# Order of the products inside a pair of experts in the first layer's MoE block

## The chip, the cores and the metric

The kernel runs on one core of a Trainium2 chip. The metric is the device time of one execution in microseconds (us), lower is better. The engines named below are TensorE (PE, matrix products and transposes), VectorE (DVE), ScalarE (ACT), GpSimd (POOL) and SyncE (SP, which here only issues loads of weights). Each engine works through its own program in the order in which it is written and meets the others at semaphores.

## The reference

A trunk of two layers over 256 latent tokens and 256 context tokens of 1024 channels. Each layer has four token mixers and then a mixture of experts (16 experts, each token goes to two of them). The context tokens go through the experts in the first layer only. What the change touches is the block of one expert:

```python
def expert_block(args):
    xblk, e = args
    u = jax.nn.silu(xblk @ w1[e]) * (xblk @ w3[e])
    return u @ w2[e]
```

with `w1` and `w3` of 1024 x 512 and `w2` of 512 x 1024, all in float32 (2048 KB each).

## The kernel before

**The experts of the first layer.** The 16 experts are taken two at a time, in 8 pairs `e`. A pair works on a main block of 64 rows (tokens) per expert and on a side block of 32 further rows per expert. The main block is multiplied by `both_halves`: the even expert's 64 rows stand in one half of the array's columns and the odd expert's in the other (L1515 and L1517, so those two lines alternate in the trace). The side block is multiplied by `four_quarters` (L1525), four products of 32 columns at a time. The first layer has the side block (`side` is true), the second has none, and takes other branches everywhere.

**A pair on PE, before:** gate product of the main block (PSUM bank 2), gate product of the side block (bank 7), up product of the main block (bank 3), up product of the side block (bank 6), then `turn_u` (four transposes of the main inner rows `u`, L1585), the low half of the down product (needs `uT`, the turned rows copied to SBUF), `turn_side_u` (L1591), the high half, and the side block's down product. PE's loop over pairs is unrolled.

**A pair on the other engines.** These programs are not in the diff. DVE: `activated` (L2718), `side_activated` (L2723 and L2725), `hidden` (L2731, writes the main inner rows and signals `u_ready`), `side_hidden` (L2735, L2738), the turning of the next pair's tokens (L2145, L2151), the results. ACT: `tanh` (L1944), `side_parts` (L1950 copies one half of the side gate product and waits for `side_gate_done`; L1952 is its tanh and waits for DVE's sum; L1954 copies one half of the side up product and waits for `side_up_done`), `turned_u` (L1958 copies the turned rows and signals `uT_ready`), the results and their stores.

**The weights.** Each of the six matrices of a pair has one place in SBUF: a place in the ring and one beside it (`n_` for `w1`, `hT` for `w3`, `wide` for `w2`). SP's loop waits for the last reader of a matrix kind, then issues the two loads of the next pair:

```python
def last_reader(w, l):
    if with_side(l):
        return {"w1": side_gate_done, "w3": side_up_done, "w2": side_down_done}[w]

for w in ("w1", "w3", "w2"):
    sp.wait_ge(last_reader(w, l), base + e)
    sp.dma_start(at[w][0], pairs_of[w][l, e, 0]).then_inc(at[w][1], 16)
    sp.dma_start(odd_at[w], pairs_of[w][l, e, 1]).then_inc(odd_landed[w], 16)
```

**The token rows** of pair `e + 1` are gathered by POOL while pair `e` is worked on.

Of the kernel before, what the change touches and what calls it, by code (L numbers as in the profile page):

```python
# [149 lines left out]
def with_side(l):  # L150

    return live(l) == TILES
# [477 lines left out]
def build_trunk(nc, xin, ccol, crows, const, cols, rows, hfw, wr, wmod, win, wbr, wout, w1, w3, w2, out):  # L630
    with ExitStack() as ctx:
# [3 lines left out]
        def sem(name):  # L635
            return ctx.enter_context(nc.semaphore(name))
# [19 lines left out]
        side_xT = yT[:, 1, 0, :].rearrange("p (k n) -> p k n", n=HALF)  # L656
# [196 lines left out]
        side_xT_ready = sem("side_xT_ready")  # L853
        side_gate_done = sem("side_gate_done")
# [11 lines left out]
        side_y_ready = sem("side_y_ready")  # L866
# [31 lines left out]
        def chunk3(name, n=KD):  # L898
            return chunk(name).rearrange("p (k n) -> p k n", k=n)
# [42 lines left out]
        def odd3(w, n=KD):  # L942

            return odd_at[w].rearrange("p (k n) -> p k n", k=n)
# [14 lines left out]
        def behind_first(l, e):  # L959

            return l or not isinstance(e, int) or e
# [168 lines left out]
        def _(pe):  # L1130
# [10 lines left out]
            for n, name in enumerate(STEPS["T"]):  # L1141
                kind, l, rest = name[0], name[1], name[2:]
# [107 lines left out]
                elif kind == "fdft":  # L1250
                    (j,) = rest
                    pe.wait_ge(vector_done, vector("fnorms", l))
                    side = 256 * (j // 2)
# [199 lines left out]
                elif kind == "experts":  # L1453
# [5 lines left out]
                    side = with_side(l)  # L1459
                    inner = u if side else eth  # L1460
                    wg, wu, wd = chunk3(("w1", l)), chunk3(("w3", l)), chunk3(("w2", l), 4)
                    wg2, wu2, wd2 = odd3("w1"), odd3("w3"), odd3("w2", 4)
# [4 lines left out]
                    def weights_landed(w, e):  # L1467
                        for two in range(2):
                            if l and ("w2", e, two) in LAST_W2 and w == "w2":
                                continue  # L1470
                            if l:
                                pe.wait_ge(*home_landed((w, e, two)))
                            elif two:
                                pe.wait_ge(odd_landed[w], e * 16 + 16)
                            else:
                                pe.wait_ge(place[w], first[w] + e * 16)
# [5 lines left out]
                    def of_pair(w, e):  # L1482
                        if l:
                            return [home_slices((w, e, two)) for two in range(2)]
                        return slices(fourths(chunk((w, l))), KD), slices(fourths(odd_at[w]), KD)
# [26 lines left out]
                    def both_halves(bnk, left, even, odd):  # L1512
                        n_k = len(even)
                        for k in range(n_k):
                            pe.matmul(ps[0:HALF, bnk, :], left[:, k, 0:HALF], even[k],  # L1515
                                      start=(k == 0), stop=(k == n_k - 1), skip_group_check=True)
                            last = pe.matmul(ps[HALF:P, bnk, :], left[:, k, HALF:P], odd[k],  # L1517
                                             start=(k == 0), stop=(k == n_k - 1), skip_group_check=True)
                        return last

                    def four_quarters(bnk, left, quarters):

                        for k in range(4):
                            for g, (weights, k0, rows_, cols_) in enumerate(quarters):
                                last = pe.matmul(ps[SIDE * g:SIDE * (g + 1), bnk, :], left[:, k0 + k, rows_:rows_ + SIDE],  # L1525
                                                 weights[:, k0 + k, cols_], start=(k == 0), stop=(k == 3),
                                                 skip_group_check=True)
                        return last

                    def split_k(even, odd):  # L1530
                        whole = slice(0, FE)
                        return [(even, 0, 0, whole), (odd, 0, SIDE, whole), (even, 4, 0, whole), (odd, 4, SIDE, whole)]
# [11 lines left out]
                    def mix(e):  # L1544

                        if not e:
                            pe.wait_ge(pieces_ready, l + 1)
                        pe.wait_ge(mixing_ready, e + 1)
                        pe.wait_ge(y_low, base + e + 1)
                        pe.wait_ge(y_high, base + e + 1)  # L1550
                        mix_block(e == 0, e == PAIRS - 1).then_inc(y_mixed, 1)

                    def gate_and_up(e):

                        pe.wait_ge(turned_low, base + e + 1)
                        if not e:
                            pe.wait_ge(turned_high, l + 1)
                        if behind_first(l, e):
                            pe.wait_ge(u_ready, base + e)
                            if side:  # L1560
                                pe.wait_ge(side_uT_ready, e)
                            if not side:
                                pe.wait_ge(y_low, base + e)
                        weights_landed("w1", e)
                        both_halves(2, xgT, *of_pair("w1", e)).then_inc(gate_done, 1)
                        if side:
                            pe.wait_ge(side_xT_ready, e + 1)
                            if behind_first(l, e):
                                pe.wait_ge(side_y_ready, e)
                            four_quarters(7, side_xT, split_k(wg, wg2)).then_inc(side_gate_done, 1)  # L1570
                        if not side and e:
                            mix(e - 1)
                        weights_landed("w3", e)
                        if not side:
                            pe.wait_ge(y_high, base + e)
                        both_halves(3, xgT, *of_pair("w3", e)).then_inc(up_done, 1)
                        if side:
                            if behind_first(l, e):
                                pe.wait_ge(y_high, base + e)
                            four_quarters(6, side_xT, split_k(wu, wu2)).then_inc(side_up_done, 1)  # L1580

                    def turn_u(e):
                        pe.wait_ge(u_ready, base + e + 1)
                        for f in range(4):
                            last = pe.transpose(ps[:, u_bank, f * P:(f + 1) * P], inner[:, f * P:(f + 1) * P], ident)  # L1585
                        last.then_inc(u_turned, 1)
# [8 lines left out]
                    def down(e):  # L1595
                        pe.wait_ge(uT_ready, base + e + 1)
                        weights_landed("w2", e)
                        if behind_first(l, e):
                            pe.wait_ge(y_low, base + e)
                        last_columns_landed(e, last_low)  # L1600
                        even, odd = of_pair("w2", e)
                        both_halves(low_bank, uT, even[0::2], odd[0::2]).then_inc(down_low, 1)
                        if side:
                            turn_side_u(e)
                        if behind_first(l, e):
                            pe.wait_ge(y_high, base + e)
                        last_columns_landed(e, last_high)
                        both_halves(high_bank, uT, even[1::2], odd[1::2]).then_inc(down_high, 1)
                        if side:
                            pe.wait_ge(side_uT_ready, e + 1)  # L1610
                            low, high = slice(0, FE), slice(FE, D)
                            four_quarters(7, side_uT, [(wd, 0, 0, low), (wd2, 0, SIDE, low), (wd, 0, 0, high),
                                                       (wd2, 0, SIDE, high)]).then_inc(side_down_done, 1)

                    def pair(e):
                        gate_and_up(e)
                        turn_u(e)
                        if side and not e:
                            pe.wait_ge(pieces_ready, l + 1)
                        down(e)  # L1620
# [25 lines left out]
                    for e in range(PAIRS):  # L1646
                        pair(e)
# [1330 lines left out]
```

## Time and profile before

| | |
|---|---|
| time, median of 3 runs (lowest to highest) | 1540.88 us (1540.47 to 1541.53) |
| time of the profiled execution | 1544.08 us |
| its span, first to last instruction | 1542.1 us |
| mean granted clock of TensorE in it | 0.989 |
| first layer's pairs of experts, from the first gate product to the end of the last side product | 663.3 to 933.1 us |
| PE busy over the span | 1445.8 us (94%) |
| DVE, ACT, POOL busy over the span | 757.9, 277.6, 165.9 us |

The profiled execution is 3.2 us above the median of the runs. The span leaves out what lies before the first and behind the last instruction. PE's busy time counts a pipelined product until its modelled end, so consecutive products overlap in the rows; the distance from one start to the next is what a product takes. Two products whose rows start together run side by side in different columns of the array.

### The profile page before, as it was taken

The numbers are of one execution on the slowest core, as the hardware profiler recorded it, in microseconds if no ns is written. First come the engines' busy times: TensorE is split into PE (matmuls) and PEld (weight loads), VectorE is DVE, ScalarE is ACT, GpSimd is POOL, SyncE is SP. The second block draws the span as 40 slices with busy tenths as digits, with TensorE's granted clock in tenths as the row PEclk, the third lists the DMA queues.
The fourth block names the chain that finished last, engine by engine and source line by source line (L and its number), as shares of the span: only waits on it lengthen the run. The fifth ranks groups of instructions, "written<-read, shape, count | busy, mean of one in ns | idle before, by whom it ended". The sixth has DMA issues, their size and how long they took to land. (4 is left out here: it accounts for less than half of the span.)

```text
span 1542.1 us, 17006 instructions
## 1 busy us (share of the span) xinstructions
PE 1445.8 (94%) x6200; PEld 718.8 (47%) x6200; DVE 757.9 (49%) x1689; ACT 277.6 (18%) x570; POOL 165.9 (11%) x156
## 2 busy tenths in 40 slices
PE   6999999789999999999999999899989999999987
PEld 2544644344444444632323233765777875433332
DVE  4297866646555879532122223686676635211112
ACT  3201101422232210411011011110242203000000
POOL 0000011001011210021111101001001210111000
PEclk9999999989999999999999999999999999999999
DMA  9420234101223453689999986425333695999996
GB/s 380 186 98 27 74 145 164 55 28 55 82 82 141 164 191 109 275 322 420 423 425 422 418 360 237 162 85 225 127 110 137 220 374 211 379 418 412 422 420 238
DMA packets 49536, 355.55 MB, mean 231 GB/s; under 512 B 6288, under 2 KB 6672, under 8 KB 22704
## 3 DMA queue, kind: packets, MB, share of 16 engines
q1 hardware_dynamic: 41360, 330.79, 54.3%
q0 software_dynamic: 4800, 14.24, 2.5%
q10 hardware_dynamic: 3296, 9.44, 1.6%
q8 instruction: 52, 0.85, 0.2%
q14 instruction: 28, 0.23, 0.0%
HBM read 343.88 MB, written 10.56 MB: 230 GB/s over the span
## 5 line engine op out<-in xcount | busy, mean ns | idle before, releaser
L1209 PE MATMUL ps<-hT,ring 128*128 128x512 f32 (+1 forms) x1344 | 452.6, 492 | 1.9 <-DVE hT L2334 1.3
L1209 PEld LDWEIGHTS ps<-hT,ring 128*128 128x128 f32 x1344 | 253.8, 192 | 177.0 <-issue 157.9
L1515 PE MATMUL ps<-ring,m 128*64 128x512 f32 x624 | 277.1, 595 | 12.7 <-ACT m L1958 8.0
L1515 PEld LDWEIGHTS ps<-ring,m 128*64 128x64 f32 x624 | 81.9, 137 | 185.4 <-issue 172.7
L2296 DVE SCALAR_TENSOR_TENSOR spare<-ring,crow 128x1024 bf16<-128x1024 f32 x120 | 155.8, 1298 | 4.1
L1222 PE MATMUL ps<-ring,hT 128*128 128x512 f32 (+1 forms) x352 | 125.1, 515 | 0.0
L2021 POOL TENSOR_TENSOR wide<-wide,gates 128x512 f32<-128x512 f32 (+1 forms) x48 | 69.6, 1450 | 395.9 <-DVE gates L2473 395.9
L1517 PE MATMUL ps<-n_,m 128*64 128x512 f32 x224 | 100.0, 595 | 0.0
L1310 PE MATMUL ps<-yT,ring 128*128 128x512 f32 (+1 forms) x256 | 94.5, 492 | 2.3 <-ACT n_ L1857 2.3
L1517 PE MATMUL ps<-wide,m 128*64 128x512 f32 x208 | 93.7, 597 | 0.0
L1222 PEld LDWEIGHTS ps<-ring,hT 128*128 128x128 f32 x352 | 66.7, 190 | 55.1 <-issue 51.4
L1517 PE MATMUL ps<-hT,m 128*64 128x512 f32 x208 | 91.9, 595 | 0.0
L2059 POOL DMA_INDIRECT m<-h_scratch,m x56 | 53.1, 949 | 348.2 <-DVE m L2145 266.5
L1393 PE MATMUL ps<-ring,wide 128*128 128x512 f32 x192 | 83.1, 593 | 1.4 <-issue 1.1
L1816 ACT ACTIVATE gates<-ps,hbg 128x512 f32<-128x512 f32 (+1 forms) x64 | 37.2, 581 | 235.3 <-PE ps L1209 149.8
L2718 DVE SCALAR_TENSOR_TENSOR m<-m,ps 128x512 f32<-128x512 f32 x16 | 11.0, 688 | 134.7 <-ACT m L1944 134.7
L2383 DVE SCALAR_TENSOR_TENSOR n_<-n_,col 128x512 f32<-128x512 f32 (+1 forms) x120 | 74.2, 619 | 4.3
L2473 DVE SCALAR_TENSOR_TENSOR gates<-gates,ps 128x512 f32<-128x512 f32 (+1 forms) x48 | 26.6, 554 | 75.1 <-PE ps L1310 67.8
L2731 DVE TENSOR_TENSOR m<-m,ps 128x512 f32<-128x512 f32 x16 | 11.0, 688 | 104.0 <-PE ps L1517 104.0
L1310 PEld LDWEIGHTS ps<-yT,ring 128*128 128x128 f32 x256 | 45.8, 190 | 32.1 <-issue 24.2
L1525 PE MATMUL ps<-ring,yT 128*32 128x512 f32 x256 | 58.1, 595 | 0.0
L1393 PEld LDWEIGHTS ps<-ring,wide 128*128 128x128 f32 x192 | 36.2, 190 | 46.3 <-issue 46.1
(389 smaller groups left out, 1699.3 us busy)
## 6 DMA issues: line engine op xcount, KB each, us to landing
ring<-w SPq DMA_DIRECT2D x39, 2048.0 KB, 11.1
ring<-win SPq DMA_DIRECT2D x52, 1024.0 KB, 4.9
ring<-wmod SPq DMA_DIRECT2D x48, 1024.0 KB, 5.0
n_<-w SPq DMA_DIRECT2D x13, 2048.0 KB
hT<-w SPq DMA_DIRECT2D x13, 2048.0 KB, 16.6
wide<-w SPq DMA_DIRECT2D x13, 2048.0 KB
ring<-wbr SPq DMA_DIRECT2D x8, 1024.0 KB, 4.8
ring<-wout SPq DMA_DIRECT2D x4, 2048.0 KB, 11.9
```

The costliest lines, as they stand in the source:

```text
L1209: last = pe.matmul(b[:, 0:W], w[:, k, jj * P:(jj + 1) * P], hT[:, k, 0:W], start=(k == 0), stop=(k == KD - 1))
L1222: last = pe.matmul(b[:, 0:wid], hT[:, k, t * P:(t + 1) * P], chunk3(parts[k // ks], ks)[:, k % ks, 0:wid], start=(k == 0), stop=(k == KD - 1))
L1310: last = pe.matmul(b[:, 0:W], w[:, k, j * P:(j + 1) * P], yT[:, bi in (1, 2), k, 0:W], start=(k == 0), stop=(k == 1))
L1393: last = pe.matmul(b, acc[:, k, t * P:(t + 1) * P], w[:, k, :], start=(k == 0), stop=(k == KD - 1))
L1515: pe.matmul(ps[0:HALF, bnk, :], left[:, k, 0:HALF], even[k], start=(k == 0), stop=(k == n_k - 1), skip_group_check=True)
L1517: last = pe.matmul(ps[HALF:P, bnk, :], left[:, k, HALF:P], odd[k], start=(k == 0), stop=(k == n_k - 1), skip_group_check=True)
L1525: last = pe.matmul(ps[SIDE * g:SIDE * (g + 1), bnk, :], left[:, k0 + k, rows_:rows_ + SIDE], weights[:, k0 + k, cols_], start=(k == 0), st ...
L1816: last = act.activation(gth[:, g % 2, 0:W], bank(("gate", l, bi, j))[:, 0:W], ACT.Tanh, bias=hbg[:, bi * 8 + j:bi * 8 + j + 1], scale=0.5)
L2021: last = nc.gpsimd.tensor_tensor(acc[:, j, 0:W], acc[:, j, 0:W], gtmp[:, g % 2, 0:W], ALU.add)
L2059: gp.indirect_dma_start(out=xg[:, 256 * g:256 * (g + 1)], out_offset=None, in_=h2_pieces, in_offset=bass.IndirectOffsetOnAxis(ap=pieces[:, ...
L2296: last = v.scalar_tensor_tensor(out=spare[:, 0, :].bitcast(BF16), in0=chunk3(cn, 2)[:, block_ % 2, :], scalar=0.5, in1=crow[:, s, :], op0= ...
L2383: last = v.scalar_tensor_tensor(out=o, in0=ud[:, j, 0:ns, k:k + 256], scalar=w(k), in1=o, op0=ALU.mult, op1=ALU.add)
```

## The change

Only PE's program changes, and only where `side` is true. Inside a pair the main block's gate and up products now come one after the other, ahead of the side block's gate product, and `turn_u` moves from behind the side block's up product to a place between the side gate product and the side up product. The waits go with their steps.

```diff
@@ gate_and_up(e)
                         weights_landed("w1", e)
                         both_halves(2, xgT, *of_pair("w1", e)).then_inc(gate_done, 1)
-                        if side:
-                            pe.wait_ge(side_xT_ready, e + 1)
-                            if behind_first(l, e):
-                                pe.wait_ge(side_y_ready, e)
-                            four_quarters(7, side_xT, split_k(wg, wg2)).then_inc(side_gate_done, 1)
                         if not side and e:
                             mix(e - 1)
                         weights_landed("w3", e)
@@
                         both_halves(3, xgT, *of_pair("w3", e)).then_inc(up_done, 1)
                         if side:
+                            pe.wait_ge(side_xT_ready, e + 1)
+                            if behind_first(l, e):
+                                pe.wait_ge(side_y_ready, e)
+                            four_quarters(7, side_xT, split_k(wg, wg2)).then_inc(side_gate_done, 1)
+                        if side:
+                            turn_u(e)
                             if behind_first(l, e):
                                 pe.wait_ge(y_high, base + e)
                             four_quarters(6, side_xT, split_k(wu, wu2)).then_inc(side_up_done, 1)
@@ pair(e)
                         gate_and_up(e)
-                        turn_u(e)
+                        if not side:
+                            turn_u(e)
                         if side and not e:
                             pe.wait_ge(pieces_ready, l + 1)
                         down(e)
```

PE's program in the second pair of the first layer, before: the first row of each product with what it waits for, in the order gate, side gate, up, side up, turn, down.

```order
L1515 MATMUL ps<-ring,m 64x512 [waits chunk_landed4,side_uT_ready,odd_w1_landed,u_ready,turned_low]
...
L1525 MATMUL ps<-ring,yT 32x512 [waits side_y_ready,side_xT_ready]
...
L1515 MATMUL ps<-ring,m 64x512 [waits odd_w3_landed,chunk_landed0]
...
L1525 MATMUL ps<-ring,yT 32x512 [waits y_high]
...
L1585 MATMUL ps<-con,m 128x128 [waits u_ready]
L1585 MATMUL ps<-con,m 128x128 x3
L1515 MATMUL ps<-ring,m 64x512 [waits odd_w2_landed,y_low,chunk_landed2,uT_ready]
```

The same place in the changed kernel, where `turn_u` is line 1586.

```order
L1515 MATMUL ps<-ring,m 64x512 [waits chunk_landed4,side_uT_ready,odd_w1_landed,u_ready,turned_low]
...
L1515 MATMUL ps<-ring,m 64x512 [waits odd_w3_landed,chunk_landed0]
...
L1525 MATMUL ps<-ring,yT 32x512 [waits side_y_ready,side_xT_ready]
...
L1586 MATMUL ps<-con,m 128x128 [waits u_ready]
L1586 MATMUL ps<-con,m 128x128 x3
L1525 MATMUL ps<-ring,yT 32x512 [waits y_high]
...
L1515 MATMUL ps<-ring,m 64x512 [waits odd_w2_landed,y_low,chunk_landed2,uT_ready]
```

The side gate product moved behind the up product, and the transposes with their wait for `u_ready` now stand directly behind the side gate product and ahead of the side up product.

DVE's program in a pair, in the changed kernel. Its rows are those of before (744 to 748 there too, with line numbers lower by two).

```order
L2720 SCALAR_TENSOR_TENSOR m<-m,ps 128x512 [waits tanh_ready]
L2725 TENSOR_TENSOR gates<-ps,gates 64x512 [waits side_gate_part]
L2727 SCALAR_TENSOR_TENSOR mr<-mr,gates 64x512 [waits side_tanh]
L2733 TENSOR_TENSOR m<-m,ps 128x512 [waits up_done,gate_ready]
L2737 TENSOR_TENSOR gates<-ps,mr 64x512 [waits side_up_copied]
```

The fourth row signals `u_ready`. Nothing moved here: it still stands behind the two rows that need the side gate product.

ACT's program in a pair, in the changed kernel, again as before but for the line numbers.

```order
L1946 ACTIVATE m<-ps 128x512 [waits gate_done]
L1952 ACTIVATE gates<-ps 64x512 [waits side_gate_done]
L1954 ACTIVATE mr<-gates 64x512 [waits side_gate_sum]
L1956 ACTIVATE mr<-ps 64x512 [waits side_up_done]
L1960 ACTIVATE m<-ps 128x512 [waits u_turned]
```

The last row signals `uT_ready`, on which the down product waits. It still stands behind the copy that needs the side up product.

## Rows read from the trace of the kernel before

**Rows 1.** Busy time by stretch, two of the pairs: PE, PEld, DVE, ACT, POOL, clock, DMA

```profile
core 0: us, PE busy (x) PEld busy (x) DVE busy (x) ACT busy (x) POOL busy (x), PEclk, DMA share, GB/s
697.30:731.10 33.80, 33.05 (x202) 10.09 (x200) 7.58 (x12) 3.61 (x6) 5.68 (x6) 1.00 1.01 423
866.10:899.80 33.70, 32.95 (x202) 10.09 (x200) 7.56 (x12) 3.61 (x6) 0.00 (x0) 1.00 1.00 422
```

**Rows 2.** Waits of PE in pairs 2 to 8 (697 to 934 us)

```profile
engine line waited for: us in total, times, longest us
PE ps L1515 <- ACT m L1958: 5.2, 7, 0.7
```

**Rows 3.** Timeline of PE, seventh pair: first product of each step

```profile
start us, us, engine line op out<-in xcount [idle before <-releaser]
865.64 0.64 PE L1515 MATMUL ps<-ring,m 128*64 128x512 f32 x1
...
872.66 0.62 PE L1525 MATMUL ps<-ring,yT 128*32 128x512 f32 x1
...
876.23 0.64 PE L1515 MATMUL ps<-ring,m 128*64 128x512 f32 x1
...
883.25 0.62 PE L1525 MATMUL ps<-ring,yT 128*32 128x512 f32 x1
...
886.82 0.66 PE L1585 MATMUL ps<-con,m 128*128 128x128 f32 x4
888.22 0.64 PE L1515 MATMUL ps<-ring,m 128*64 128x512 f32 x1 [0.75 <-ACT m L1958]
...
899.35 0.64 PE L1515 MATMUL ps<-ring,m 128*64 128x512 f32 x1
```

**Rows 4.** Timeline of ACT, seventh pair

```profile
876.37 0.59 ACT L1950 ACTIVATE gates<-ps 64x512 f32<-64x512 f32 x1 [2.99 <-PE ps L1525]
877.71 0.63 ACT L1952 ACTIVATE mr<-gates 64x512 f32<-64x512 f32 x1 [0.75 <-DVE gates L2723]
886.95 0.59 ACT L1954 ACTIVATE mr<-ps 64x512 f32<-64x512 f32 x1 [8.62 <-PE ps L1525]
887.57 0.60 ACT L1958 ACTIVATE m<-ps 128x512 f32<-128x512 f32 x1
```

**Rows 5.** Timeline of DVE, seventh pair

```profile
876.99 0.68 DVE L2723 TENSOR_TENSOR gates<-ps,gates 64x512 f32<-64x512 f32 x1 [2.90 <-ACT gates L1950]
878.37 0.68 DVE L2725 SCALAR_TENSOR_TENSOR mr<-mr,gates 64x512 f32<-64x512 f32 x1 [0.69 <-ACT mr L1952]
883.43 0.69 DVE L2731 TENSOR_TENSOR m<-m,ps 128x512 f32<-128x512 f32 x1 [4.38 <-PE ps L1517]
```

**Rows 6.** Loads of weights by SP: issues in the seventh pair, then landing times, all pairs

```profile
876.50 0.33 SPq L1074 DMA_DIRECT2D ring<-w  x1
...
886.95 0.33 SPq L1074 DMA_DIRECT2D ring<-w  x1
...
899.48 0.33 SPq L1074 DMA_DIRECT2D ring<-w  x1
...
DMA to landing us min/median/max: 7.9/10.8/11.6
...
DMA to landing us min/median/max: 15.6/16.4/17.3
```

**Rows 7.** Timeline of PE: a transpose behind a wait for DVE's inner rows, second layer

```profile
1357.43 0.66 PE L1585 MATMUL ps<-con,m 128*128 128x128 f32 x4 [1.23 <-DVE m L2731]
```

**Rows 8.** Timeline of PE: the first product behind some of its longest waits

```profile
10.10 1.94 PE L1157 MATMUL ps<-ring,cc 128*32 128x512 f32 x8 [4.02 <-DMA ring<-wmod]
...
307.82 1.29 PE L1331 MATMUL ps<-m 32*128 32x256 f32 x4 [4.71 <-ACT n_ L1857]
...
935.41 2.46 PE L1168 MATMUL ps<-con 128*128 128x512 f32 x4 [2.27 <-issue]
...
1504.86 0.61 PE L1515 MATMUL ps<-ring,m 128*64 128x512 f32 x1 [2.56 <-DMA hT<-w]
```

**Rows 9.** Busy time by stretch, behind these waits (columns as in Rows 1)

```profile
10.10:13.50 3.40, 2.95 (x16) 0.40 (x16) 1.13 (x4) 1.70 (x2) 0.00 (x0) 1.00 1.05 432
307.82:312.00 4.18, 4.18 (x8) 1.98 (x9) 2.70 (x8) 1.59 (x5) 0.00 (x0) 0.50 0.00 0
...
936.63:940.04 3.41, 3.41 (x14) 0.60 (x16) 0.50 (x3) 0.00 (x0) 0.94 (x1) 0.51 0.00 0
...
1504.86:1508.30 3.44, 3.44 (x16) 1.40 (x18) 0.00 (x0) 0.00 (x0) 0.00 (x0) 1.00 0.97 414
```

## The prediction

> **What bounds the kernel now.** I read the waits first, because the changed stage looks full on two resources at once. The table of stretches shows a pair of experts taking 33.7 us with PE busy for 33.0 of them at full clock, and in the same stretch the DMA share at 1.00 and 422 GB/s [rows 1]. So both PE and the transfers of weights could be the bound, and they would give opposite forecasts. The waits of PE decide it: in pairs 2 to 8 its only one is for ACT's copy of the turned rows, 7 times, 0.7 us each [rows 2]. PE never waits for a weight there. The landing times say by how much: in the seventh pair the two loads of `w1` are issued from 876.50, those of `w3` from 886.95, those of `w2` from 899.48, and the second load of each kind lands 15.6 to 17.3 us behind its issue [rows 6]. Its `w1` is wanted by the next gate product at 899.35 [rows 3], 22.4 us behind the issue of its second load at about 877.0. Five microseconds are left even at the longest landing. PE's own program is what a pair takes, although the DMA engines are busy all the time.
>
> The second thing to see is the order of the seventh pair on PE, by the starts of its steps [rows 3]: gate 865.64, side gate 872.66 (the main gate product takes 7.02), up 876.23 (side gate 3.57), side up 883.25 (up 7.02), turn 886.82 (side up 3.57), down 888.22, next pair 899.35. That is 33.71 us.
>
> The third is what the up product hides. When the side gate product ends, a chain of hand-overs begins: ACT copies (876.37), DVE adds (876.99), ACT takes the tanh (877.71), DVE finishes at 878.37 + 0.68 = 879.05 [rows 4, 5]. Only then can DVE go on to `hidden`, which makes the inner rows. In the kernel before PE has 7 us of up product meanwhile, and `hidden` waits for that product (883.43 [rows 5]); behind it lies another 3.6 us of side up product before PE asks for the inner rows. So the chain costs nothing now.
>
> **The change, part by part.**
>
> *Side gate product behind the up product.* The same 16 steps of products, moved past others of the same engine; by itself 0 on PE. But it puts the start of the hand-over chain 7 us later in the pair, behind both main products.
>
> *`turn_u` directly behind the side gate product.* It waits for `u_ready`. `hidden` stands on DVE behind the two operations that need the side gate product, and the order of DVE's program is unchanged. So PE now waits out the whole chain with nothing beside it. From the rows: side gate product's end (the next start, 876.23) to ACT's copy 0.14; from there to the end of DVE's second operation 2.68 (876.37 to 879.05); `hidden` itself 0.69, with a step of 0.04 before it as between neighbouring DVE operations; and 0.04 from DVE to PE (my estimate of such a hand-over, from the links between ACT and DVE in [rows 4, 5], of which the three shown took 0.03 to 0.04 each). Sum **3.59 us** of wait per pair. The up product that `hidden` also needs has long ended.
>
> *The transposes.* They took no time on the path before: they lay under ACT's copy of the side up product, since the copy that releases the down product stands on ACT behind that one (886.95 + 0.59, then 887.57 + 0.60, then down at 888.22) [rows 3, 4]. In their new place they are on the path. The four are busy for 0.66 [rows 7], as in [rows 3]; products overlap the end of what is ahead of them by about 0.06, so I take **0.60 us**.
>
> *Behind the side up product.* One could hope that the down product now starts at once, as its rows are turned early. It doesn't: ACT's copy (`turned_u`) stands behind its copy of the side up product, so both still follow the end of that product and the distance from the side up start to the down start stays at 888.22 - 883.25 = 4.97 us [rows 3]. **0 us** gained. The Trainium skill ("TensorE: Matmul & The Clock Gate", section "Architectural detail: the array is 16x 32x32, not 1x 128x128") says that ScalarE and VectorE are strictly first in, first out. No row here can show an overtaking that never came up; if ACT could take the second copy first, the 1.4 us would be saved and a pair would cost 2.8 more instead of 4.2.
>
> *The queues.* SP's wait for `side_gate_done` comes 7 us later in a pair, so `w1` is issued 17.9 us into a pair of 37.9 instead of 10.9 into 33.7. That leaves 37.9 - 18.4 = 19.5 us for its second load; the longest landing was 17.3 [rows 6]. `w3`: side up ends at 25.4, wanted 7.0 into the next pair, 19.0 us for the second load. Both hold with the queue as full as now, and it will be emptier, since the same bytes are spread over a longer pair. Behind SP's later wait only the loads of `w3` and `w2` are queued, whose own conditions come later still. POOL's gathers hang on DVE's turning of the tokens, which stays where it was against the side up product. Cost 0; if the slack were short by a few us, each pair would pay that.
>
> *The first pair and the end.* In the first pair the up product starts 3.6 us earlier, at about 670.4. I leave it at no cost. Behind the last pair the stores, the gathers and the second layer all follow its end, so the whole delay is passed on. The second layer's program is unchanged.
>
> Sum of orders alone: (3.59 + 0.60) x 8 = **33.5 us**.
>
> **The clock.** A wait of 3.6 us that recurs in each pair also bears on PE's clock. This is a cost that the stage doesn't show now (granted 1.00 in it [rows 1]), so I bound it. Behind a wait of 4.02 us the clock stayed at 2.4 GHz, behind one of 4.71 it was at 1.2 GHz for the whole of a 4.18 us stretch; behind one of 2.27 it fell (1.2 GHz from 936.63 to 940.04), behind one of 2.56 it did not [rows 8, 9]. So at this length it can go either way, and it is not the length alone that decides. Lower bound: no fall, 0. A fall like that of 936.63 lasts 3.41 us; half of it is lost if PE has work, 1.7 us. Upper bound: in each of 8 pairs a low stretch twice as long, 8 x 3.41 = 27 us. I take a fall in 7 of 8 pairs at 1.7 us, **11.9 us**, nearer to the falls because PE's pauses in a pair add up: 3.6 us, and another 1.3 us only 4.2 us later. The Trainium skill (same page, section "HAM oscillation — how this bites in real kernels") describes a loop whose wait between two bursts of products sends the clock down in every turn and prices it at half of the low time. By that rule it would be all eight pairs, 13.6 us, and the forecast 1588; this trace agrees for the waits of 4.71 and 2.27 us and not for those of 4.02 and 2.56.
>
> **Sum.** 33.5 + 11.9 = 45.4 us. The durations are of an execution of 1544.08 us and the runs' median is 1540.88; the difference of 0.2% doesn't matter to durations of 4 us. 1540.9 + 45.4 = **1586.3 us**, 2.9% slower.
>
> **Rivals.**
>
> 1. *The clock holds.* Only the waits and the transposes are paid: 1540.9 + 33.5 = 1574.4. For it: 1.00 in all pairs now, and the 4.02 us wait. Against: the fall behind 2.27 us.
> 2. *The clock falls longer.* Each low stretch is 6 to 7 us instead of 3.4, as the one of the 4.71 us wait was longer than 4: 1540.9 + 33.5 + 27 = 1601.4.
> 3. *The transfers are the bound and absorb it.* With the DMA share at 1.00 a pair could be set by its 14.2 MB (33.7 us at 422 GB/s), and a PE wait would only fill slack: 1541. For it: [rows 1]. Against: [rows 2], where PE waits for no load, and the 5 us of slack.
> 4. *Faster.* If the inner rows were ready when the side gate product ends, the early turn would take ACT's copy and the transposes out of the path to the down product: the 1.4 us from 886.82 to 888.22 [rows 3], 8 times, 11 us, so 1530. It decides at a chain of at most nothing behind the side gate product and a copy on ACT ahead of that of the side up product; the program order has neither.
> 5. *Late weights.* If landing took over 19 us, a few us per pair on top: 3 x 8 = 24 over the forecast of the clock that holds, 1598. Against: the slack above.
>
> **How the numbers follow.** Forecast (falls in about 5 to 8 pairs, single length) 0.62; rival 1 with at most four falls 0.22; rival 2 0.08; rival 5 0.03; rival 3 0.03; rival 4 0.01; anything else 0.01. The low end of the range is rival 1 less 3 us for clock falls elsewhere in the second layer that may go or come with the shift (1571), the high end takes in most of the way to rival 2 (1598). A measurement of this kernel can tell about 0.2% (3 us) from no change. Faster 0.01, same 0.03 (rival 3), slower 0.96.
>
> **What would show it.** In the changed profile: eight waits of PE for DVE's `hidden` (L2733 there) at the transposes (L1586), 3.6 us each, total 28 to 29; the wait for ACT's copy ahead of the down product grows from 0.75 to about 1.3 since the transposes no longer fill part of it; a pair of 37.9 us at full clock, up to 39.6 with a fall; DMA at 370 GB/s or less in the stage; a granted clock below 1.00 in most pairs. The prediction is wrong if the wait at the transposes is much shorter than 3 us (something on DVE or ACT runs ahead), if PE waits for loads in the stage, or if the second layer gives part of it back.

## The result and the profile after

| | before | changed |
|---|---|---|
| time, median (lowest to highest), 6 runs each | 1541.47 us (1540.47 to 1546.84) | 1584.39 us (1582.26 to 1588.37) |
| ratio, 95% interval | | 1.0263, 1.0243 to 1.0283 |
| profiled execution: time, span, granted clock | 1544.08, 1542.1 us, 0.989 | 1585.68, 1583.7 us, 0.982 |
| stage of the pairs, first gate product to the next step's first product | 663.33 to 935.41, 272.1 us | 663.99 to 976.66, 312.7 us |

The change makes the kernel 2.6% slower. Two executions of the later runs, 2598.9 us in experiment 5 and 1938.4 us of the kernel before beside it, ran in a slow state of the chip and are left out of every median and ratio below. Of the 41.6 us between the two spans, 40.6 lie in the stage of the eight pairs.

The waits of PE in the changed kernel, from 697 us (pairs 2 to 8; pair 1 has the same waits before that), answer to [rows 2]:

```profile
engine line waited for: us in total, times, longest us
PE ps L1586 <- DVE m L2733: 23.9, 7, 3.4
PE ps L1515 <- ACT m L1960: 9.4, 7, 1.3
```

A wait for DVE's inner rows has appeared at the transposes, 3.4 us in every pair, and the wait ahead of the down product has grown from 0.7 to 1.3 us, because the transposes no longer fill part of it. PE still waits for no load. The timeline of PE in the fourth pair, whose clock was full, against [rows 3]:

```profile
781.35 0.64 PE L1515 MATMUL ps<-ring,m 128*64 128x512 f32 x1
...
788.27 0.59 PE L1515 MATMUL ps<-ring,m 128*64 128x512 f32 x1
...
795.24 0.62 PE L1525 MATMUL ps<-ring,yT 128*32 128x512 f32 x1
...
802.28 0.66 PE L1586 MATMUL ps<-con,m 128*128 128x128 f32 x4 [3.40 <-DVE m L2733]
802.87 0.62 PE L1525 MATMUL ps<-ring,yT 128*32 128x512 f32 x1
...
807.85 0.64 PE L1515 MATMUL ps<-ring,m 128*64 128x512 f32 x1 [1.34 <-ACT m L1960]
...
818.97 0.64 PE L1515 MATMUL ps<-ring,m 128*64 128x512 f32 x1
```

From the side gate product's start to the transposes it is 7.04 us, where the product itself takes 3.57: 3.47 of wait. The transposes take 0.59 until the next product. The two main products take 13.89 together instead of 14.04. The pair takes 37.62 us instead of 33.71. DVE in the sixth pair shows the chain that PE waits for ([rows 5] for before):

```profile
876.51 0.68 DVE L2725 TENSOR_TENSOR gates<-ps,gates 64x512 f32<-64x512 f32 x1 [9.77 <-ACT gates L1952]
877.89 0.68 DVE L2727 SCALAR_TENSOR_TENSOR mr<-mr,gates 64x512 f32<-64x512 f32 x1 [0.70 <-ACT mr L1954]
878.50 0.67 DVE L2733 TENSOR_TENSOR m<-m,ps 128x512 f32<-128x512 f32 x1
```

`hidden`, the last of these rows, now runs straight behind the side block's second operation; before, 4.4 us of idle DVE lay ahead of it. The busy time by pair adds the clock (columns as in [rows 1]):

```profile
702.98:742.30 39.32, 34.58 (x204) 10.53 (x200) 7.48 (x11) 3.61 (x6) 5.69 (x6) 0.96 0.90 362
742.30:781.35 39.05, 34.30 (x204) 10.62 (x200) 7.48 (x11) 3.61 (x6) 5.68 (x6) 0.96 0.89 362
781.35:818.97 37.62, 32.88 (x204) 10.18 (x200) 7.48 (x11) 3.61 (x6) 5.68 (x6) 1.00 0.89 365
818.97:858.29 39.32, 34.58 (x204) 10.53 (x200) 7.49 (x11) 3.61 (x6) 5.68 (x6) 0.96 0.92 371
```

Two of the eight pairs, the fourth and the seventh, ran at 1.00 and took 37.6 us; in each of the six others the clock fell once to 1.2 GHz for 3.41 us, so they show 0.96, and took 39.0 to 39.4. The DMA share has fallen from 1.00 to about 0.90.

### The profile page after: what moved, and what is told of

It reads as the page before. It is cut to its first block and busy times, and to the rows that moved or that the text cites. A ratio compares the mean times of both kernels' runs of the same rounds, so it can differ in the third digit from the quotient of the medians.

```text
span 1583.7 us, 17006 instructions
## 1 busy us (share of the span) xinstructions
PE 1454.0 (92%) x6200; PEld 721.3 (46%) x6200; DVE 757.2 (48%) x1689; ACT 277.6 (18%) x570; POOL 165.8 (10%) x156
## 5 line engine op out<-in xcount | busy, mean ns | idle before, releaser
L1515 PE MATMUL ps<-ring,m 128*64 128x512 f32 x624 | 275.4, 595 | 17.3 <-ACT m L1960 12.1
L1525 PE MATMUL ps<-ring,yT 128*32 128x512 f32 x256 | 66.1, 663 | 0.0
```

What stands on the lines that cost most here:

```text
L1515: pe.matmul(ps[0:HALF, bnk, :], left[:, k, 0:HALF], even[k], start=(k == 0), stop=(k == n_k - 1), skip_group_check=True)
```

## The experiments

All times are medians; each ratio is against the kernel before, measured beside it on the same chip, whose median was 1544.6 to 1547.1 us there. "Stage" is the time from the first gate product to the product behind the last pair, 272.1 us in the kernel before and 312.7 us in the changed one.

**1. Transposes last.** The changed kernel with `turn_u` where it was.

```diff
                         if side:
-                            turn_u(e)
                             if behind_first(l, e):
@@ pair(e)
-                        if not side:
-                            turn_u(e)
+                        turn_u(e)
```

> The changed order of the products (main gate, main up, side gate, side up), but the transposes back behind the side up product. Theory W (the time went into PE's wait for the inner rows behind the side gate product, the transposes in the open and the clock falls that the wait causes): the side up product of 3.57 us covers the chain of hand-overs of 3.4 us, the wait at the transposes is under 0.2 us, the clock stays at 1.00 in the stage, and the time is that of before, 1537 to 1545 us. Rival O (the swap of the products itself costs, by later release of w1 and later loads): the time stays within 5 us of the changed kernel, 1580 to 1589 us.

Measured: 1586.5 us, ratio 1.0276 (1.0250 to 1.0302), stage 310.0 us. Theory W had the wait at the transposes right and the time wrong. The waits of PE in the stage:

```profile
PE ps L1515 <- DMA hT<-w: 25.9, 7, 4.8
PE ps L1515 <- ACT m L1958: 4.9, 7, 0.7
```

The wait for the inner rows is gone, and a wait for the second load of `w3` (into `hT`) stands in its place: 3.6 to 4.8 us in pairs 2 to 7 and 0.8 in the last, 3.7 on average. SP's loads and PE's up product of one pair:

```profile
761.56 0.33 SPq L1074 DMA_DIRECT2D ring<-w  x1
762.08 0.33 SPq L1075 DMA_DIRECT2D n_<-w  x1
764.86 0.33 SPq L1074 DMA_DIRECT2D ring<-w  x1
765.29 0.39 SPq L1075 DMA_DIRECT2D hT<-w  x1
...
789.12 1.09 PE L1515 MATMUL ps<-ring,m 128*64 128x512 f32 x1 [4.77 <-DMA hT<-w]
```

The loads of `w1` and `w3` are issued 3.3 us apart. Here is the landing time of the second `w3` load issued at 765.29 (the number at the end), whose end is PE's start:

```profile
hT<-w SPq DMA_DIRECT2D x1, 2048.0 KB, 23.7
```

In the kernel before the issues were 10.4 us apart and no second load of `w3` took over 17.3 us [rows 6]. In the pair of these loads nothing moves for almost 3 us ahead of the release of `w1` (first row), and over the whole of the next pair DMA's busy share is down to 0.85 (second row; columns as in [rows 1]):

```profile
758.70:761.50 2.80, 2.80 (x32) 0.82 (x28) 0.00 (x0) 0.07 (x1) 0.00 (x0) 1.00 0.00 0
...
777.26:818.05 40.79, 35.31 (x205) 11.04 (x201) 7.48 (x11) 3.61 (x6) 5.67 (x6) 0.92 0.85 348
```

So the queue runs dry until `w1` is released, and is then asked for the loads of `w1` and `w3` almost at once. The load waits make 25.9 of the 38.0 us that this stage is over the kernel before; much of the rest goes with the clock, which was granted 0.91 to 0.96 in pairs 2 to 7. This is rival O's cost, by a mechanism that theory W had put at nothing. From here on the theory is M: two bounds side by side, of which a pair pays the longer.

**2. Early transposes, old order of products.** The kernel before with `turn_u(e)` between the main up and the side up product.

```diff
                         both_halves(3, xgT, *of_pair("w3", e)).then_inc(up_done, 1)
                         if side:
+                            turn_u(e)
@@ pair(e)
-                        turn_u(e)
+                        if not side:
+                            turn_u(e)
```

> The products in the order of before (main gate, side gate, main up, side up), but the transposes between the main up and the side up product. Theory W: the side gate product is long done, the inner rows only wait for the up product, a wait of 0.8 to 0.9 us at the transposes plus 0.6 us of transposes in the open, 8 times, 12 us: 1549 to 1556 us, and no clock falls in the stage. Rival O: as the products keep their order, no more than 5 us over before, 1541 to 1546. A third theory, that an early turn costs the same wherever it stands: near 1584.

Measured: 1555.9 us, ratio 1.0066 (1.0045 to 1.0087), stage 284.2 us, 12.1 over before. Its waits in the whole stage hold 8 at the transposes:

```profile
PE ps L1586 <- DVE m L2733: 6.9, 8, 0.9
```

As theory W said: the early turn costs 1.5 us per pair when it waits for the up product alone, 0.86 of wait and 0.59 of transposes in the open, and the clock stays at 1.00 in all eight pairs.

**3. A filled wait, too full.** Seven identity products ahead of the transposes of the changed kernel.

```diff
                         if side:
+                            for _ in range(7):
+                                pe.matmul(ps[:, 0, :], ident, ident.unsqueeze(1).broadcast_to([P, 4, P]),
+                                          start=True, stop=True)
                             turn_u(e)
```

> The changed kernel with seven products of the identity (3.0 us at full clock, into a PSUM bank that nothing else uses in this stage) between the side gate product and the transposes in each pair. They give no result that is read. Theory W with its clock term: the wait at the transposes shrinks to 0.4 us, the granted clock is 1.00 in the stage, and the pairs still take 37.6 us, so the time falls by the clock's share alone, 8 to 11 us: 1573 to 1577. Rival: the clock falls cost nothing that isn't hidden, time within 3 us of the changed kernel (1581 to 1588).

Measured: 1599.4 us, ratio 1.0355 (1.0330 to 1.0380), stage 324.1 us. A product of this kind takes 0.87 us, two rows of 0.43 each, where I had counted one, so seven took 6.1 us and overran the wait by 2.6 us. The expected time was missed by that error, and the time says nothing on what the falls of the clock cost.

**4. Inner rows first.** The changed kernel with `hidden` ahead of the side block's operations on DVE.

```diff
                         activated(e)
+                        hidden(e)
                         if side:
                             side_activated(e)
-                        hidden(e)
```

> The changed kernel with one edit on DVE: the operation that makes the main inner rows stands ahead of the two operations on the side gate product. Theory W: the inner rows are ready while the side gate product runs, no wait at the transposes, no falls; what stays is the transposes in the open (0.58 us) less 0.16 us per pair that two main products in a row save, 3.4 us in all: 1543 to 1547. Rival O: 1575 or more. If the copy on ACT behind the side up product were what holds the pair, nothing would change from 1584.

Measured: 1582.2 us, ratio 1.0253 (1.0227 to 1.0279); in the profiled run, which was the fastest of its five, the stage took 301.6 us. Theory W, which forecast 1543 to 1547, missed again: the wait at the transposes is gone, and as in experiment 1 the load took its place. Here the issues of `w1` and `w3` are 4.0 us apart, and the second load of `w3` took 22.0 to 23.4 us wherever PE waited for it.

```profile
PE ps L1515 <- DMA hT<-w: 20.9, 6, 4.5
```

**5. A filled wait.** As experiment 3 with `range(3)`.

> The changed kernel with three identity products instead of seven in the wait (in the run before this one a product of this kind took 0.87 us, not 0.43, so seven overran the wait; three take 2.6 us). Theory W with its clock term: the wait at the transposes shrinks from 3.4 to 0.8 us, the granted clock is 1.00 in the stage, the pairs all take 37.6 us, and the time is that of the changed kernel less the six clock falls, 1572 to 1577 us. Rival: the falls cost nothing of their own, 1582 to 1588.

Measured: 1578.2 us (median of three), ratio 1.0214 (1.0182 to 1.0247), stage 303.5 us. Its pairs:

```profile
738.42:776.05 37.63, 35.65 (x210) 11.25 (x206) 7.48 (x11) 3.61 (x6) 5.68 (x6) 1.00 0.92 375
888.95:926.58 37.63, 35.65 (x211) 11.25 (x208) 7.48 (x11) 3.61 (x6) 0.00 (x0) 1.00 0.93 380
```

Each pair behind the first takes 37.6 us at full clock, with the same chain on DVE and ACT. In the stage that is 312.7 - 303.5 = 9.1 us less than in the changed kernel. The median is 1 us above the expected range. The ratio lies 0.5% (8 us) under the changed kernel's, with intervals that just overlap, so the times alone leave the clock's share uncertain; it is the stage, with the clock at 1.00 in each of its pairs, that shows it.

**6. Lighter loads.** Three kernels with the first half of each `w1` matrix only, in pairs 2 to 8: the changed kernel, experiment 1 and experiment 4.

```diff
+                                n = WCH // 2 if w == "w1" else WCH
-                                sp.dma_start(at[w][0], pairs_of[w][l, e, 0]).then_inc(at[w][1], 16)
-                                sp.dma_start(odd_at[w], pairs_of[w][l, e, 1]).then_inc(odd_landed[w], 16)
+                                sp.dma_start(at[w][0][:, 0:n], pairs_of[w][l, e, 0][:, 0:n]).then_inc(at[w][1], 16)
+                                sp.dma_start(odd_at[w][:, 0:n], pairs_of[w][l, e, 1][:, 0:n]).then_inc(odd_landed[w], 16)
```

> The changed kernel, but of pairs 2 to 8 of the first layer only the first half of each w1 matrix is loaded (the other half keeps the first pair's weights, so the experts' results are not the reference's). Theory M (two bounds stand side by side, and a pair takes the longer: the chain of hand-overs at the transposes, and the loads that can only begin once the side gate product has released w1): in the changed kernel the chain is the longer one and PE waits for no load, so lighter loads change nothing: 1580 to 1589. If the loads set the changed kernel's time in any hidden way: below 1575.

> The first experiment (changed product order, transposes last) with the same halved loads of w1. Theory M: there PE waited 4 to 5 us per pair for the second load of w3, which stood in the queue behind both loads of w1; with 2 MB less in front of it, it lands 5 us earlier, the wait is gone or under 1 us per pair, and the time is 1538 to 1548 us. If the product order cost through something on PE itself, the time stays near 1586.

> The fourth experiment (changed kernel with the inner rows made ahead of the side gate's operations on DVE) with the same halved loads of w1. Theory M: with both bounds taken away only the transposes in the open remain, 1541 to 1549 us. If the early turn costs in some other way: 1570 or more.

| kernel | full loads | half of `w1` |
|---|---|---|
| changed | 1.0263 (1.0243 to 1.0283) | 1584.9 us, 1.0245 (1.0214 to 1.0275) |
| experiment 1 | 1.0276 (1.0250 to 1.0302) | 1545.3 us, 0.9989 (0.9976 to 1.0002) |
| experiment 4 | 1.0253 (1.0227 to 1.0279) | 1549.8 us, 1.0024 (1.0006 to 1.0042) |

The changed kernel doesn't feel its loads. The two others fall to the kernel before (experiment 4's 1 us above its expected range), the one with the transposes in the open 4.5 us above the other, for 8 x 0.59 = 4.7 us of transposes. In experiment 1 with light loads no second load of `w3` took over 17.2 us again, and a pair took 33.4 us:

```profile
DMA to landing us min/median/max: 14.2/16.5/17.2
...
698.05:731.47 33.42, 32.72 (x205) 10.28 (x201) 7.49 (x11) 3.61 (x6) 5.67 (x6) 1.00 0.90 363
```

**7. The copy first.** The changed kernel with one edit on ACT, and the changed kernel again beside it.

```diff
                         act.activation(side_act, side_gate, ACT.Tanh, scale=0.5).then_inc(side_tanh, 1)
+
+                    def side_up_half(e):
                         act.wait_ge(side_up_done, e + 1)
@@ pair(e)
                         turned_u(e)
+                        if side:
+                            side_up_half(e)
```

> The changed kernel with one edit on ACT: the copy of the turned rows stands ahead of its copy of the side up product. The prediction held that this order, and not the place of the transposes, keeps 1.4 us between the side up and the down product. If so that wait is gone (0.1 us or less), a pair takes 36.3 instead of 37.6 us at full clock and the time falls by 8 to 11 us against the changed kernel in the same job. If the loads then come too late (the second load of w3 has 17.5 us left, and took up to 17.4 in the changed kernel), part of it comes back as waits of PE for them: 3 to 8 us. If the order on ACT doesn't matter: within 2 us.

> The changed kernel once more, unedited, as the measure for the run beside it and for the filled wait before: 1.0245 to 1.0275 of the kernel before.

Measured: 1575.4 us, ratio 1.0183 (1.0144 to 1.0222), against 1586.8 us, 1.0266 (1.0234 to 1.0297) unedited: 11 us less. The wait ahead of the down product is gone and PE waits for no load. Its only large wait in the stage:

```profile
PE ps L1586 <- DVE m L2737: 27.3, 8, 3.4
```

But the pairs take 37.55 us, not 36.3, because the clock now fell in each of the eight:

```profile
738.64:776.20 37.56, 34.15 (x205) 10.60 (x202) 7.36 (x11) 3.61 (x6) 5.67 (x6) 0.95 0.93 380
776.20:813.75 37.55, 34.14 (x205) 10.62 (x201) 7.36 (x11) 3.61 (x6) 5.67 (x6) 0.95 0.93 375
```

**8. A version from these pieces.** The kernel before, its order of products kept, with the transposes in the middle of the side up product and ACT's edit of experiment 7.

```diff
-                    def four_quarters(bnk, left, quarters):
+                    def four_quarters(bnk, left, quarters, halfway=None):
                         for k in range(4):
+                            if halfway and k == 2:
+                                halfway()
@@ gate_and_up(e)
-                            four_quarters(6, side_xT, split_k(wu, wu2)).then_inc(side_up_done, 1)
+                            four_quarters(6, side_xT, split_k(wu, wu2), lambda: turn_u(e)).then_inc(side_up_done, 1)
@@ pair(e)
-                        turn_u(e)
+                        if not side:
+                            turn_u(e)
```

> From the kernel before, its order of products kept: the transposes stand in the middle of the side up product, and ACT copies the turned rows ahead of its copy of the side up product. Theory M: half a side up product (1.8 us) covers the 0.9 us chain behind the up product, the 1.4 us between side up and down products vanish, 0.6 us of transposes come into the open, so PE alone would need 32.9 instead of 33.7 us per pair; the loads, at 14.2 MB per pair and 423 to 425 GB/s, need 33.4 us, so 0.3 to 0.8 us per pair are saved: 0 to 6 us, 0.0% to 0.4% under the kernel before. Rival: the loads already set the pace of the kernel before, then within 0.1% of it, with waits of PE for loads in the stage. Third: the later release of w3 by the transposes (0.6 us) makes it slower by up to 5 us.

Measured: 1539.5 us against 1545.4, ratio 0.9965 (0.9947 to 0.9983), stage 266.6 us. A pair takes 33.0 us, all of it with PE busy:

```profile
825.24:858.27 33.03, 33.03 (x204) 9.99 (x200) 7.45 (x11) 3.61 (x6) 5.68 (x6) 1.00 1.01 422
```

It beats the kernel before by 0.35%. The bound of 33.4 us that I had put on the loads did not show within eight pairs; that the slack was being used up meanwhile is my reading of the longest landing of a second load, that of `w3`, which was 15.1 us in the first pair, 19.8 in the sixth and 18.6 in the seventh, and no run shows more.

## Why the prediction was right, and where it wasn't

The forecast of 1586.3 us and the range held, and for the changed kernel each step shows in its trace:

- *What bounds the kernel.* That PE and not the loads set a pair before the change holds; experiment 8 took 0.7 us out of PE's part of each pair, and the pairs became 0.7 us shorter.
- *The chain at the transposes.* Forecast 3.59 us, measured 3.47 to 3.48. The links were as priced, but `hidden` began 0.07 us before the end of the operation ahead of it (878.50 against 877.89 + 0.68), not 0.04 behind it.
- *The transposes in the open.* Forecast 0.60, measured 0.59.
- *Two main products in a row* save 0.15 us, which the forecast had at 0. The orders alone: 37.62 - 33.71 = 3.91 us per pair, 31.3 in all, where 33.5 was forecast.
- *Nothing gained behind the side up product,* since the copy on ACT stands behind another. Experiment 7 shows it: only when ACT's order is changed are the 1.3 us gone. The Trainium skill ("TensorE: Matmul & The Clock Gate", "Architectural detail: the array is 16x 32x32, not 1x 128x128") has ScalarE as strictly first in, first out; this pair of traces agrees: the copy of the turned rows, with its input ready, still came behind that of the side up product, 1.34 us of wait, and only the other order in ACT's program took that to 0.
- *The clock.* Forecast 7 falls at 1.7 us, 11.9; measured 6 falls and 9.1 us (the changed stage less that of experiment 5). A fall cost between 1.4 us (39.05 - 37.62) and 1.7 us (39.32 - 37.62), the smaller where part of the low stretch lay in the wait: in that pair the transposes right behind it took 1.11 us, where [rows 7] has 0.66. The rule of the Trainium skill ("TensorE: Matmul & The Clock Gate", "HAM oscillation — how this bites in real kernels"), a fall in every turn of the loop at half of the low time, was right for experiment 7's kernel in count (8 of 8) and not in price (1.3 us each, 37.55 less the 36.28 that are 37.62 without the wait of 1.34, where half of 3.41 would be 1.7), and in count for six pairs of eight of the changed kernel.

```profile
763.24 1.11 PE L1586 MATMUL ps<-con,m 128*128 128x128 f32 x4 [3.41 <-DVE m L2733]
```

- *A clock reading that was wrong.* The forecast took it from the first row of [rows 9] that the clock stayed at 2.4 GHz behind the wait of 4.02 us. The clock records of that trace begin only at 32.2 us, and a stretch without a record shows as 1.00. The products themselves speak against it: behind that wait eight of them took 1.94 us [rows 8], 1.06 us each, and 29 us later sixteen of the same line and shape took 1.92, 0.59 to 0.62 us each:

```profile
38.82 1.92 PE L1157 MATMUL ps<-ring,cc 128*32 128x512 f32 x16
```

So the eight ran at half the pace, that of 1.2 GHz; whether the clock had fallen in the wait or had not yet risen at all, this wait was no evidence for rival 1 or against the Trainium skill's rule. The waits of 2.27 us with a fall and 2.56 us without one still show that the length alone doesn't decide. Seven falls was thus a choice between bounds, and that six came is near to it partly by luck.

Sum in the stage: 31.3 + 9.1 = 40.4 of the measured 40.6 us.

The step that failed is the first of "The change, part by part", that the side gate product behind the up product costs "0 on PE", with its part on the queues, "Cost 0". For the changed kernel as a whole the number stands: its second loads of `w3` took at most 17.4 us and had 19. (The 15.6 to 17.3 us of [rows 6] are theirs alone too, not those "of each kind": the landings of the second `w1` and `w2` loads are not in that trace.) But the argument, "Both hold with the queue as full as now, and it will be emptier", took the landing time for a property of the load. It depends on how far apart the loads are issued. With the loads of `w1` and `w3` released 3.3 us apart (experiment 1) the latter took 23.7 us. In the changed kernel they were 9.0 us apart in a pair with a fall of the clock, and 7.5 us in one at full clock:

```profile
876.02 0.33 SPq L1074 DMA_DIRECT2D ring<-w  x1
...
884.97 0.33 SPq L1074 DMA_DIRECT2D ring<-w  x1
...
799.08 0.33 SPq L1074 DMA_DIRECT2D ring<-w  x1
...
806.57 0.33 SPq L1074 DMA_DIRECT2D ring<-w  x1
```

and what spaces them, next to the side up product's own 3.57 us, is the very wait for the inner rows, with the transposes and the low clock. Even so the load of the full-clock pair landed 17.4 us behind its issue, 1.4 us before PE wanted it. So the swap of the products alone costs as much as the whole change (1.0276 against 1.0263); with the swap in place the early turn adds nothing, while without it it costs 0.66% (experiment 2); and undoing one of the two waits gives nothing back. Each hides under the other; experiment 6 separates them, since light loads free experiments 1 and 4 and leave the changed kernel where it is. My sum was right because it counted the wait for the inner rows, and the late loads were covered by it. That the two are of nearly the same size is chance, and nothing in the forecast knew of it. Rival 5 named the mechanism of late weights and its point, 19 us; I gave it 0.03 as a property of the changed kernel and didn't see that it lay right behind the wait.

Rival 1 (the clock holds) was true of two pairs of eight; experiment 5 shows the kernel that it describes. Rivals 2, 3 and 4 fell: no low stretch of the stage was a double one in the changed kernel, nothing was absorbed, and the down product did not start earlier.

## What to carry to other kernels

Where a weight has one place in SBUF, the order of products is also the order in which loads are released: moving a buffer's last reader later bunches the loads, and the one behind lands later, here 24 instead of 17 us behind its issue with the same bytes. Before a stall is blamed for a loss, take it away: if another wait of the same size appears, the stage has two bounds, and both have to be undone together. To start a step earlier, its input has to be ready by then and the copy behind it has to move as well: with the transposes 1.8 us behind the up product and ACT's copy moved (experiment 8), the early turn gains 0.35%; directly behind the up product and with ACT's order left (experiment 2) it costs 0.66%.

## What was unexpected

- A wait of 3.41 us, the same in each pair to 0.01 us, lowered the clock in six pairs of eight in the changed kernel, in eight of eight in experiment 7, while its pairs settled at 37.55 us each. What decides it between waits of the same length stays open here.
- An identity product of 128x512 in float32 takes 0.87 us, as two rows of 0.43 us, like the steps of the kernel's own products (7.02 us for eight).
